# Walking the columns of the second and third feed-forward input matmuls as interleaved streams

## The reference, cut to what matters

```
def swiglu(h, w_in, w_out):
    gt, up = jnp.split(h @ w_in, 2, axis=-1)
    return (jax.nn.silu(gt) * up) @ w_out

for l in range(DEPTH):                      # DEPTH = 2
    ...
    h = adaln_pre(x, mod[:, 0], norm_pre[l, 0])
    x = adaln_post(x, swiglu(h, ffn_w_in[l, 0], ffn_w_out[l, 0]), mod[:, 0], norm_post[l, 0], 0.5)
    ...                                     # token mixing
    h = adaln_pre(x, mod[:, 2], norm_pre[l, 2])
    x = adaln_post(x, swiglu(h, ffn_w_in[l, 1], ffn_w_out[l, 1]), mod[:, 2], norm_post[l, 2], 0.5)
```

## Time and profile before

| | |
|---|---|
| median of 2 runs | 2431.36 us (2428.53 and 2434.2) |
| span of the profiled execution | 2428.7 us |
| TensorE busy | 2382.6 us, 98% of the span |
| VectorE, ScalarE, GpSimd busy | 51%, 41%, 5% |
| mean granted TensorE clock | 0.996 of full speed |
| matmuls in the program | 18,794 |
| of these, in whole-width steps of in1 and in2 | 2 x 28 x 48 = 2,688 |

### The profile page before, as it was taken

One profiled execution on the slowest core, in us unless ns is written; L12 is line 12 of the kernel. 1 busy time (PEld: TensorE's weight loads), 2 busy tenths in 40 slices (PEclk: granted clock), 3 DMA queues, 4 the chain that ended last, 5 costly groups with the idle time before them and its releaser, 6 DMA issues.

```text
span 2428.7 us, 43792 instructions
## 1 busy us (share of the span) xinstructions
PE 2382.6 (98%) x18794; PEld 2185.1 (90%) x18794; DVE 1241.6 (51%) x1725; ACT 995.2 (41%) x1399; POOL 115.2 (5%) x232
## 2 busy tenths in 40 slices
PE   6999999999999999999999999999999999999998
PEld 5999999965599999999999999887777999999998
DVE  5533346755576333367533347755554758633245
ACT  4522234625466222346522235533223546522243
POOL 0000000122100000000000000012222100000000
PEclk9999999999999999999999999999999999999999
DMA  8555345774536653565754255544555455632254
GB/s 306 175 184 189 114 158 179 254 216 126 189 118 226 217 165 99 185 208 174 264 181 164 83 167 183 190 157 162 172 165 165 133 177 181 206 129 88 87 179 155
DMA packets 122658, 417.09 MB, mean 172 GB/s; under 512 B 23386, under 2 KB 27610, under 8 KB 122210
## 3 DMA queue, kind: packets, MB, share of 16 engines
q1 hardware_dynamic: 89538, 302.08, 38.8%
q10 hardware_dynamic: 17568, 61.87, 7.2%
q0 software_dynamic: 15360, 50.34, 6.3%
HBM read 390.84 MB, written 23.41 MB: 171 GB/s over the span
## 4 chain that ended last, share of the span: by engine, by line
PE 87%; DVE 5%; DMA 3%; ACT 3%; issue 2%; SPq 1%; POOLq 0%; POOL 0%; ACTq 0%; DVEq 0%
PE PS L2030 71%; PE PS L1425 3%; PE PS L1964 2%; PE PS L1994 2%; DVE WL L2316 2%; PE PS L1355 1%; DMA RAW<-in_w_in 1%; ACT WH L2142 1%; PE PS L1309 1%; PE PS L1340 1%; PE PS L1350 1%; PE PS L1321 1%; PE PS L791 1%; PE PS L1404 1%; PE PS L794 1%
## 5 line engine op out<-in xcount | busy, mean ns | idle before, releaser
L2316 DVE TENSOR_TENSOR WL<-RAW,WH 128x1024 fp32r<-128x1024 f32 (+1 forms) x478 | 633.1, 1325 | 648.7 <-ACT WH L2142 648.0
L2030 PE MATMUL PS<-HH,WH 128*128 128x260 f32 x3432 | 796.5, 285 | 2.4 <-ACT SG L2262 0.7
L2030 PE MATMUL PS<-HH,WL 128*128 128x260 f32 x3432 | 786.5, 283 | 0.0
L2030 PE MATMUL PS<-HL,WH 128*128 128x260 f32 x3368 | 769.6, 283 | 0.0
L2142 ACT ACTIVATE WH<-RAW 128x1024 fp32r<-128x1024 f32 (+1 forms) x478 | 542.0, 1135 | 424.7 <-PE PS L2030 264.9
L2030 PEld LDWEIGHTS PS<-HH,WH 128*128 128x128 f32 x3432 | 569.9, 188 | 24.7 <-issue 16.8
L2030 PEld LDWEIGHTS PS<-HH,WL 128*128 128x128 f32 x3432 | 569.4, 188 | 0.0
L2030 PEld LDWEIGHTS PS<-HL,WH 128*128 128x128 f32 x3368 | 557.0, 188 | 0.6 <-issue 0.2
L2030 PE MATMUL PS<-GH,WH 128*128 128x260 f32 x1408 | 386.1, 284 | 0.2
L2030 PE MATMUL PS<-GL,WH 128*128 128x260 f32 x1408 | 384.2, 283 | 0.0
L2030 PE MATMUL PS<-GH,WL 128*128 128x260 f32 x1408 | 383.5, 283 | 0.0
(11 more groups left out here) (338 smaller groups left out, 2320.0 us busy)
## 6 DMA issues: line engine op xcount, KB each, us to landing
RAW<-in_w_in SPq DMA_DIRECT2D x236, 512.0 KB, 3.6
RAW<-in_w_out SPq DMA_DIRECT2D x120, 704.0 KB, 4.0
AW<-in_w_ada ACTq DMA_DIRECT2D x114, 512.0 KB, 5.6
RAW<-in_w_odd SPq DMA_DIRECT2D x60, 512.0 KB, 3.7
RAW<-in_w_odout SPq DMA_DIRECT2D x30, 512.0 KB, 3.8
RAW<-in_w_even SPq DMA_DIRECT2D x28, 512.0 KB, 4.3
KV<-in_v_pages POOLq DMA_DIRECT2D x32, 256.0 KB, 5.0
SR<-in_ret_past POOLq DMA_DIRECT2D x32, 256.0 KB, 3.9
```

What stands on the lines that cost most here:

```text
L2030: last = nc.tensor.matmul(ps[:, x, 0:HT], w[:, k * P:(k + 1) * P], src[k0 + k][:, x, :], start=(begin and t == 0), stop=(end and t == 2))
L2316: nc.vector.tensor_tensor(low_, RAW[:, from_:from_ + w], high_.bitcast(F32), ALU.subtract).then_inc(lo_done, 1)
```

## The change

The moving operand and the result of each matmul in a whole-width step of in1 and in2 are given as a rearranged view. The set of elements is the same, and each moving column still lands in the PSUM column of the same number; only the order in which the 260 columns are walked differs, and it differs in the same way on both sides.

- in1: the 260 columns are cut into 2 streams of 130 and walked as pairs: columns 0, 1, 130, 131, 2, 3, 132, 133, and so on. That is 130 runs of 2 elements (8 bytes).
- in2: the 260 columns are cut into 5 streams of 52 and walked as fours: columns 0 to 3, 52 to 55, 104 to 107, 156 to 159, 208 to 211, 4 to 7, and so on. That is 65 runs of 4 elements (16 bytes).

```
+            def streams(p, hs, ap):
+
+                if hs == BOTH and STAGE_OF[p] == "in1":
+                    return ap.rearrange("p (a b c) -> p b a c", a=2, c=2)
+                if hs == BOTH and STAGE_OF[p] == "in2":
+                    return ap.rearrange("p (a b c) -> p b a c", a=5, c=4)
+                return ap
+
             def products(p, ps, xh, xl, k0, n, hs, first, last_k, b=None, chunk_ok=None, span=None, order=None,
                          ready=None, middle=None):
@@
                     for t, (w, src) in enumerate(((high, xh), (high, xl), (low, xh))):
                         for x in range(hs.start, hs.stop):
                             last = nc.tensor.matmul(
-                                ps[:, x, 0:HT], w[:, k * P:(k + 1) * P], src[k0 + k][:, x, :],
-                                start=(begin and t == 0), stop=(end and t == 2))
+                                streams(p, hs, ps[:, x, 0:HT]), w[:, k * P:(k + 1) * P],
+                                streams(p, hs, src[k0 + k][:, x, :]), start=(begin and t == 0), stop=(end and t == 2))
```

## The result

The changed kernel takes 2526.47 us (median of two, 2524.24 and 2528.7) against 2431.36: a ratio of 1.0391, 95% interval 1.0373 to 1.0409. It is slower by 95 us, inside the range of 2424 to 2567 us, but the forecast was no change. Both walks cost time, the pairs nearly three times as much as the fours.

A forecast was written before the change was run, and what follows sets the result against it. The prediction took TensorE's matmul pitch to bound in1 and in2. Both walks were priced at 0, so 2428.7 + 0 + 0 = 2428.7 us profiled, or 2431 us against the median of 2431.36; range 2424 to 2567 us.

The forecast's parts named there:

- What bounds the kernel: Whole-width steps of in1 and in2: TensorE always busy, so time is matmul pitch, 120 ns, times matmul count.
- the price of the walk: In1 and in2 whole-width matmuls: both new walks cost 0 ns, the lower end of 0 to 101 ns a matmul.
- The unexplained 0.033 ns a column: Contiguous matmuls: a pitch of 0.45 ns a column against 0.417 ns at 2.4 GHz, the difference left unexplained.
- small-price rival: In1's pairs alone pay for changes between groups of four: 8.6 ns a matmul, 12 us, 2443 us; chance 0.07.
- Pairs halve the rate, fours don't: In1's pairs use half of each four-element group, at most 221 ns a matmul; in2 free; 2564 us; chance 0.13.
- Each jump costs about a column: In1's 129 and in2's 64 jumps cost 0.45 ns each, 117 us in all, 2548 us; chance 0.05.
- Every walk at half rate: In1 and in2 both run at half rate for any non-contiguous walk, 272 us together, 2703 us; chance 0.14.

## Why the prediction was wrong, point by point

**What bounds the kernel: right.** "Whatever the new order adds to the pitch is paid in full" held to a few per cent: 1,344 x 71.3 ns = 95.8 us of pitch gave 95.1 us of median. Instruction counts, weight loads, readers and splits stayed as costed, at nothing; the waits for TensorE only grew, as said (L2262's in in1 from 46.5 us to 79.4). The half-width steps and output stages kept their pitch (144 half-width matmuls of in1 take 17.46 us before and after).

**The step that failed is the price of the walk.** I took 0 ns for both, on the ground that L1359, the one walk with a jump, costs nothing. Measured are 52.4 ns for the pairs and 18.9 ns for the fours, 70.4 and 25.4 us in place of 0 and 0. The row was read correctly and transferred wrongly, for three reasons. First, L1359 is a plain-float32 stream at 0.84 ns a column. There even 256 visits in pairs cost only 15 ns of 429, because the floor of a visit lies under the slow stream. The fp32r stream at 0.45 ns a column has no such room. Second, L1359's two runs start at multiples of four columns, so it goes to 128 aligned groups, just as many as a contiguous 512 columns; the edit's pairs go to a group 130 times instead of 65. Of that price the row could show nothing. Third, the fours go to 65 groups as before and pay for the jumps alone: 18.9 ns for 64 jumps is 0.3 ns a jump. One such jump can't be seen in a row whose two instructions are given to 0.01 us together, 5 ns each. "Nothing that these rows resolve" was a bound of some ns a jump, and I carried it over to 129 and 64 jumps as 0.

**I looked at the wrong side.** The text says the forecast hangs on "what a run of 2 or 4 elements costs on the result side". The result side is free in all walks tried. The moving side, on which I thought I had a row, carries the whole price.

**The unexplained 0.033 ns a column was the clue.** The prediction gives a rate of 0.45 where it takes 0.417 ns from the clock, and passes over the difference, except in the small-price rival. In the fit below it is the floor itself: 65 groups x 1.80 ns = 117 ns against 108 ns for 260 columns at 0.417 ns (an estimate from the granted clock; the shortest pitch measured for 260 columns is 113.1 ns). The contiguous walk already stood at the floor, and more groups could not be had for nothing. The other reading of the rate lies in the earlier trace rows: 233 ns for 128 groups and 121.5 for 65 give 1.77 ns a group, as well as 0.45 ns a column. The rows fitted both readings and I took one.

**The rivals.** *Pairs halve the rate, fours don't*: pairs took 174 ns, not 221, and fours weren't free. *Each jump costs about a column* gave 58 and 29 ns, 2548 us; measured are 52 and 19, 2526 us. It is the nearest in time, and its mechanism is wrong for the pairs: they cost 2.8 times the fours and not twice, the result's jumps cost nothing, pairs from five streams cost 147 ns for the same 129 jumps, and 259 jumps of single columns gain 8. *Every walk at half rate*: falls with the fours. *The small price*, 12 us, had the right origin, the change from one group of four to the next, and was much too small; fours were to be free by it and cost 25 us. That the time lies inside the range is luck: the upper end, 2567, was drawn for pairs at half rate, and what happened is none of the cases that the range was made of.

**The Trainium skill's two rules.** SBUF — State Buffer, section Door 1, holds that two hits in a 16-byte line suffice to hide its latency, and also that each access that crosses to a new line pays a penalty. The prediction took up the first half alone. These runs bear out the second: an aligned group of four 4-byte columns, 16 bytes, is the unit that counts on the moving side, and each one more costs about 2 ns. They don't bear out the number two. Two columns of a group cost as much as four where each visit is a new group (233.7 ns for 130 visits), and even the contiguous walk is held back, 8.4 ns of 121.5. PSUM — Partial Sum Buffer, section Specifications (TRN2), holds that any non-contiguous pattern slows matmuls significantly. For the result side no run here bears it out: pairs and fours stay at 121.5 ns and, in plain float32, single columns at 429 ns.

## What fits all the walks

Take 4.5 ns for each matmul and 1.80 ns for each group that a lane passes to. Both come from the rows of 256 and 260 contiguous columns, 119.7 and 121.5 ns, which differ by one group and little time, so they are an estimate; for 512 contiguous columns, 128 groups, they give 235 ns, and the earlier trace rows have 233. With the number of visits of one lane counted, the cost of a visit, (pitch - 4.5) / visits, comes out as:

| walk on the moving side | visits | pitch ns | ns a visit |
|---|---|---|---|
| contiguous, 256 and 260 columns | 64, 65 | 119.7, 121.5 | 1.80 |
| contiguous from column 2, 256 columns | 65 | 121.6 | 1.80 |
| 0, 2, 1, 3 and so on | 65 | 121.5 | 1.80 |
| runs of 26, of 10, two streams | 70, 78 | 131.9, 148.2 | 1.82, 1.84 |
| runs of 32, of 8, two streams | 64 | 120.8, 124.9 | 1.82, 1.88 |
| fours: 2, 3, 4, 5, 13 streams | 64, 63, 64, 65, 65 | 128.3, 127.7, 137.7, 140.4, 138.3 | 1.93, 1.96, 2.08, 2.09, 2.06 |
| pairs 4 apart; singles 2 apart | 130 | 233.7, 233.7 | 1.76, 1.76 |
| pairs: 5, 13, 10 streams | 130 | 268.1, 268.4, 256.2 | 2.03, 2.03, 1.94 |
| singles: 10, 26 streams | 130 | 265.9, 268.0 | 2.01, 2.03 |
| pairs: 4, 3, 2, 2 streams (256, 252, 256, 260 columns) | 128, 126, 128, 130 | 227.5, 188.1, 167.8, 173.9 | 1.74, 1.46, 1.28, 1.30 |
| fours across two groups, two streams | 128 | 170.9 | 1.30 |
| singles: 4 streams | 128 | 143.4 | 1.09 |
| four columns a lane from each group (256, 260 columns) | 32, 33 | 113.0 to 113.1 | held by another floor |

A visit costs about 1.8 ns in order and up to 2.1 after a jump. The three rows before the last are cheaper. In all of them a lane comes back to a group that it had shortly before, which I take for the cause. How that discount works is open: it falls from two streams to five, and it is larger where the lane comes back three times (singles from four streams) than once. The two lanes are the simplest picture that I found for all rows; what is shown is that the times come out if every other column is counted together, not what there is in the chip. Not tried: other element types, so whether four columns or 16 bytes are the unit is open as well.

## What to carry to other kernels

For an fp32r matmul with a moving operand of some 260 columns, the time is set by the aligned groups of four columns (16 bytes) that the walk takes from SBUF, about 1.8 ns for each in order and up to 2.1 after a jump, less where a walk soon comes back to a group. The contiguous walk is already at that floor; keep moving operands aligned and contiguous, or weave two streams of single columns so that every other column stays in its group. Put a permutation on the side of the result or of its readers, where it was free in all that was tried. Before a row is used as a bound for something faster, ask whether its own slower rate hides what is to be priced, and how large a price one case of it could hide when the change makes a hundred. And don't pass over a rate that misses the clock by 8%.

## What the runs showed of the hardware that I had not expected

- A contiguous fp32r walk isn't the fastest one: 121.5 ns for 260 columns against 113.1 for two woven streams of single columns, and 92 us of a kernel of 2434 hang on it when all its feed-forward and output stages are woven.
- 256 columns that begin in the middle of an aligned group cost as much as 260 that begin at its start (121.6 and 121.5 ns).
- A result walked in PSUM as pairs, fours or (plain float32) single columns from two streams costs nothing: 121.5 and 429 ns, as before.
- ScalarE's and VectorE's reads of every second column of PSUM cost nothing: 603 and 695 ns against 605 and 696. This one was expected, but no row of before showed it.
- 224 contiguous columns take 113.0 ns, as much as the woven 256 and 260 (113.0 and 113.1).
